# A decoder layer on one core: the first attention runs its token tiles two together instead of one after another

## The reference, cut to what matters

```python
# forgetting attention, 6 heads of 64 ("f"), for tokens t of a tile and all s <= t
s = q @ k.T * scale + cum[t] - cum[s];  o_f = softmax(s) @ v
# sparse attention, 6 query heads on 2 kv heads: three branches, each softmaxed by itself, gated and added
o_c = p_c @ vc                 # "c": 31 compressed keys
o_s = softmax(q @ k_slc.T * scale - slope * dist) @ v_slc    # "s": all blocks are selected at 512 tokens
o_w = softmax(q @ k_win.T * scale - slope * dist) @ v_win    # "w": window of 512
o = g0 * o_c + g1 * o_s + g2 * o_w
# all heads side by side, then the output projection
x = x + concat(o_f, o_pool, o) @ w_out
```

## Time and profile before

| what | us |
|---|---|
| median of 3 runs (815.58 to 817.59) | 815.82 |
| the profiled execution, its own time | 814.84 |
| its span (first to last instruction) | 813.0 |
| attention, first score to first matmul of the output projection | 156.49 to 259.92 |

### The profile page before, as it was taken

One profiled execution on the slowest core, in us unless ns is written; L12 is line 12 of the kernel. 1 busy time (PEld: TensorE's weight loads), 2 busy tenths in 40 slices (PEclk: granted clock), 3 DMA queues, 4 the chain that ended last, 5 costly groups with the idle time before them and its releaser, 6 DMA issues.

```text
span 813.0 us, 11870 instructions
## 1 busy us (share of the span) xinstructions
PE 765.6 (94%) x4244; PEld 595.0 (73%) x4244; DVE 534.8 (66%) x734; ACT 464.6 (57%) x697; POOL 181.2 (22%) x173
## 2 busy tenths in 40 slices
PE   3999999999999999999999986999999999999991
PEld 3978789666676889888798866677777777777761
DVE  4445346476677345632364289888899898899975
ACT  4455633376677315632353061687778887877852
POOL 2920000000000102000000010224555544455332
PEclk9999999999999999999999996999999999999996
DMA  9835440000006533553101767799999999999936
GB/s 291 228 86 151 135 130 2 0 1 2 1 2 201 188 129 107 190 196 101 55 1 52 266 235 294 289 394 371 386 385 380 370 381 373 375 387 382 384 106 220
DMA packets 61663, 167.23 MB, mean 206 GB/s; under 512 B 7926, under 2 KB 35894, under 8 KB 49334
## 3 DMA queue, kind: packets, MB, share of 16 engines
q1 hardware_dynamic: 56376, 150.69, 50.1%
q0 software_dynamic: 4240, 12.80, 6.7%
q10 hardware_dynamic: 1008, 3.21, 1.2%
HBM read 153.42 MB, written 13.24 MB: 205 GB/s over the span
## 4 chain that ended last, share of the span: by engine, by line
PE 52%; DMA 18%; POOL 10%; DVE 8%; issue 7%; ACT 4%; POOLq 1%; SPq 0%; ACTq 0%; DVEq 0%
DMA xod<-tok,yidx 16%; PE ps L1733 11%; PE ps L1735 11%; PE ps L1734 11%; POOL yidx L742 7%; PE ps L1941 5%; PE ps L1917 3%; PE ps L1981 2%; PE ps L1963 2%; PE ps L1936 2%; PE ps L1820 2%; POOL tok L753 1%; DVE wlo L1204 1%; POOL spare L750 1%; DVE wlo L1212 1%
## 5 line engine op out<-in xcount | busy, mean ns | idle before, releaser
L1204 DVE TENSOR_TENSOR wlo<-raw,whi 128x2048 fp32r<-128x2048 f32 x30 | 68.8, 2292 | 104.5 <-ACT whi L824 104.5
L1733 PE MATMUL ps<-whi,mhi 128*96 128x512 f32 (+1 forms) x288 | 114.2, 397 | 2.6 <-DVE mlo L1666 1.2
L1735 PE MATMUL ps<-whi,mlo 128*96 128x512 f32 (+1 forms) x288 | 113.6, 394 | 0.0
L1734 PE MATMUL ps<-wlo,mhi 128*96 128x512 f32 (+1 forms) x288 | 112.9, 392 | 0.0
L693 POOL TENSOR_SCALAR stat<-stat 128x1 f32<-128x1 f32 x18 | 11.5, 642 | 448.0 <-ACT tok L843 298.6
L1212 DVE TENSOR_TENSOR wlo<-arena,whi 128x2048 fp32r<-128x2048 f32 x40 | 91.5, 2291 | 14.9 <-ACT whi L837 14.9
L837 ACT ACTIVATE whi<-arena 128x2048 fp32r<-128x2048 f32 x40 | 76.7, 1917 | 28.6 <-PE ps L1735 28.6
L824 ACT ACTIVATE whi<-raw 128x2048 fp32r<-128x2048 f32 x30 | 57.3, 1910 | 62.3 <-PE ps L1735 62.2
L1733 PE MATMUL ps<-ahi,whi 128*128 128x512 f32 x192 | 76.2, 397 | 0.0
L1735 PE MATMUL ps<-ahi,wlo 128*128 128x512 f32 x192 | 75.3, 392 | 0.0
L1734 PE MATMUL ps<-alo,whi 128*128 128x512 f32 x192 | 75.3, 392 | 0.0
(11 more groups left out here) (334 smaller groups left out, 1657.6 us busy)
## 6 DMA issues: line engine op xcount, KB each, us to landing
arena<-in_exp_w_gate SPq DMA_DIRECT2D x30, 1024.0 KB, 18.0
arena<-in_exp_w_up SPq DMA_DIRECT2D x17, 1024.0 KB, 17.9
raw_a<-in_exp_w_down SPq DMA_DIRECT2D x16, 1024.0 KB, 20.1
raw<-in_exp_w_up SPq DMA_DIRECT2D x15, 1024.0 KB, 18.3
arena<-in_exp_w_down SPq DMA_DIRECT2D x9, 1024.0 KB, 21.9
raw<-in_exp_w_down SPq DMA_DIRECT2D x7, 1024.0 KB, 20.1
raw<-in_w_in SPq DMA_DIRECT2D x5, 1024.0 KB, 5.9
raw<-in_w_in SPq DMA_DIRECT2D x10, 512.0 KB, 5.7
```

The lines of the kernel that those rows point to most:

```text
L1204: v.tensor_tensor(wlo[:, n % SPLIT, :], raw[:, n % RAW, :], whi[:, n % SPLIT, :].bitcast(F32), ALU.subtract).then_inc(lo_done, 1)
L1733: mm(out_, ahi_, bhi_, start=first, stop=False)
L1734: mm(out_, ahi_, blo_, start=False, stop=False)
L1735: return mm(out_, alo_, bhi_, start=False, stop=last)
```

## The change

`TILES_A` becomes (3, 0, 2, 1), and the unit list is built for tiles 3 and 0 together, then for tiles 2 and 1 together. In each half the `f` pairs come first and alternate between the two tiles (two units of tile 3, two of tile 0, and so on), then all four `c` units, then for each pair of heads: s, s, w, w of the one tile and s, s, w, w of the other. The number of units, their instructions and their sizes stay. The bookkeeping that was written as arithmetic for one tile after another (`out_of`, `place`, the waits for a tile's outputs and for `PTc`) becomes tables made from the list: `jobs`, `spots`, `last_s`, `tile_outs`. The last `f` score is now unit 51 of 80 instead of unit 67. The lags (3 and 5 units) and the numbers of buffers are as before.

```diff
--- before.py
+++ after.py
@@ -244,7 +244,7 @@
         win, wout = A["w_in"][0], A["w_out"][0]
         wq, wk, wv, wo = (A[f"xattn_w{c}"][0] for c in "qkvo")
 
-        TILES_A = tuple(range(NT - 1, -1, -1))
+        TILES_A = (3, 0, 2, 1)
         pieces = []
         groups = []
         KEY = {}
@@ -355,9 +355,10 @@
 
 
         UN = []
-        for i in TILES_A:
-            UN += [(i, "c", g, 0) for g in range(NSA_G)] + [(i, "f", h, i + 1) for h in range(FOX_H)]
-            UN += [(i, b, 2 * p + e, i + 1) for p in range(NSA_H // 2) for b in "sw" for e in range(2)]
+        for both in (TILES_A[0:2], TILES_A[2:4]):
+            UN += [(i, "f", 2 * p + e, i + 1) for p in range(FOX_H // 2) for i in both for e in range(2)]
+            UN += [(i, "c", g, 0) for i in both for g in range(NSA_G)]
+            UN += [(i, b, 2 * p + e, i + 1) for p in range(NSA_H // 2) for i in both for b in "sw" for e in range(2)]
         UX = [(i, "x", h, MT) for i in range(NT) for h in range(MEM_H)]
 
 
@@ -387,6 +388,14 @@
                 self.o_lo = sem(name + "_o_lo")
                 self.by = 2 if name == "A" else 1
                 self.njobs = n // self.by
+                pairs = [units[u] for u in self.of_s][1::2]
+                self.jobs, self.spots, self.last_s = [], [], {}
+                for j, (i, kind, h, nb) in enumerate(pairs if self.by == 2 else ()):
+                    if kind != "w":
+                        self.spots.append((i, h // 2 if kind == "f" else 5 + h // 2))
+                    if kind == "s":
+                        self.last_s[i] = j
+                    self.jobs.append((len(self.spots) - 1, kind != "w", kind != "s"))
                 self.outs = 6 if name == "A" else MEM_H
                 self.steps = len(units) + LAG_V + 1
 
@@ -401,10 +410,13 @@
 
                 if self.by == 1:
                     return j, True, True
-                i, r = divmod(j, 9)
-                if r < 3:
-                    return 6 * i + r, True, True
-                return 6 * i + 3 + (r - 3) // 2, r % 2 == 1, r % 2 == 0
+                return self.jobs[j]
+
+            def tile_outs(self, t):
+
+                if self.by == 1:
+                    return self.outs * (t + 1)
+                return max(q for q, (i, f) in enumerate(self.spots) if i == t) + 1
 
             def bank(self, q):
 
@@ -418,14 +430,11 @@
 
             def place(self, q):
 
-                i, p = divmod(q, self.outs)
-                if self.by == 2:
-                    i = TILES_A[i]
-                t = slice(i * P, (i + 1) * P)
                 if self.by == 1:
-                    return slice(2 * p, 2 * p + 2), t
-                f = p if p < 3 else p + 2
-                return slice(f, f + 1), t
+                    i, p = divmod(q, self.outs)
+                    return slice(2 * p, 2 * p + 2), slice(i * P, (i + 1) * P)
+                i, f = self.spots[q]
+                return slice(f, f + 1), slice(i * P, (i + 1) * P)
 
         PA = Phase("A", UN, 0)
         PX = Phase("X", UX, 72)
@@ -1017,8 +1026,8 @@
                         i, kind, h, nb = ph.units[u]
                         act.wait_ge(ph.tp_done, u + 1)
                         if kind == "c":
-                            if TILES_A.index(i) >= 2:
-                                act.wait_ge(ph.pv_done, 9 * (TILES_A.index(i) - 2) + 8)
+                            if i in TILES_A[2:]:
+                                act.wait_ge(ph.pv_done, ph.last_s[{2: 0, 1: 3}[i]] + 1)
                             dst, src = PTc[i % 2][h], ps[3 + u % 2][0:NSA_R * CMP_PAD, 0:P]
                         else:
                             s = ph.sidx[u]
@@ -1769,7 +1778,7 @@
                     if ORDER[n] in ("out0", "xo0"):
 
                         ph = PA if ORDER[n] == "out0" else PX
-                        pe.wait_ge(ph.o_lo, ph.outs * ((TILES_A.index(idx) if ph is PA else idx) + 1))
+                        pe.wait_ge(ph.o_lo, ph.tile_outs(idx))
                     if kind == "H":
                         tc = slice(idx * P, (idx + 1) * P)
                         h4, l4 = (x[:, n % SPLIT, :].rearrange("p (k n) -> p k n", k=KF) for x in (whi, wlo))
```

## The result

The changed kernel takes 818.34 us, the kernel before 815.46 in the same comparison (16 runs each): a ratio of 1.0041, with a 95% interval of 1.0027 to 1.0054, so 2.2 to 4.4 us slower, 3.3 by the ratio and 2.9 between the two medians. The forecast was 819.4, 3.6 slower.

The account below looks back on a forecast made before the run. PE, busy 94%, bounds the kernel, so only idle time could move. Waits summed to 9.15 us against 4.7 before, +4.5, but the step-by-step walk's +3.6 was taken: 815.82 + 3.6 = 819.4 us, range 815.9 to 821.5.

Parts of the forecast that it names:

- The walk of PE's steps: Attention, step by step from piece prices and three wait rules: ends at 107.0 us against 103.4 before, +3.6.
- Only idle time can move: Attention: PE's instructions stay, so only its idle time can change, 4.7 us in all before the change.
- Start, 1.2: First half's start: small third and fourth scores leave PE waiting 0.7 for a score bank and 0.45 for scaling.
- Rule C: Transposes of unit k-3 wait for unit k-5's copy out of the same bank, done behind the exponential of score k-2.
- rival 2: Attention: only scaling and score banks hold PE, not copies; ends at 105.1 us, +1.6, 817.4 in all; chance 0.18.
- Forgetting units, 0.9: First half's `f` units: waits of 0.5 at step 6 and 0.4 at step 11; a gain of about 1 us over before.
- Gap, 1.3: First half's four `c` units, steps 12 to 15, without scores: transposes 9, 10, 11 wait 0.15, 0.75, 0.4 us.
- Refill, 2.1: First half, steps 16 to 23 behind the `c` units: waits at steps 19 to 22 of 0.35, 0.65, 0.95, 0.15 us.
- Steady groups: `s` and `w` units: PE sets the pace, 11.03 us per first-half group plus waits of 0.2 and 0.15; second half none.
- Rival 1: Attention: mixing works as meant, only start and drain cost, 1.2 + 0.4 for 4.7: -3.1 us, 812.7; chance 0.07.
- Rival 3: Attention: the clock falls in the gaps, 1.5 us lost over 4 us, +3 for both on top, 822.4; chance 0.05.
- Rival 4: Behind the attention: something waits for a transfer, so the attention changes but the end doesn't move, 815.8; chance 0.06.

Follow-up runs that it names:

- e1: The changed kernel with three PSUM banks for the transposes and two for the outputs: attention 104.66 us, ratio 1.0016 to the kernel before.
- e3: The changed kernel with the four `c` units of each half ahead of its `f` units: attention 103.84 us, ratio 1.0002 to the kernel before.
- e4: The changed kernel with each half's `c` units spread, one ahead of each four `f` units and one behind the last: attention 105.60 us, ratio 1.0027.
- e2: The kernel before with three PSUM banks for the transposes and two for the outputs: attention 102.45 us, ratio 0.9989 to the kernel before.
- e6: The changed kernel with both `c` units first in each half and three transposition banks: attention 101.38 us, ratio 0.9987 to the kernel before.
- e5: The changed kernel with neighbouring tiles together (TILES_A = 3, 2, 1, 0): attention 105.20 us with the clock fallen inside, ratio 1.0009 to the kernel before.

## Why the prediction was right

The walk of PE's steps ended at 107.0; the attention took 106.93. The mechanism held: gaps and refills at the compressed units, with PE waiting for ACT's copies. That the end was met to 0.1 is luck beside that, for single terms miss by up to 0.4. By its steps:

- *Only idle time can move.* Held: 4244 matmuls in both, and all of +3.50 in the attention, carried on 1:1 (553.1 and 553.4 behind it).
- *Start, 1.2.* Held to 0.02 (fourth score and first transposes above).
- *Rule C.* Held: PE starts 0.05 behind the end of each copy in the four places shown. e1 shows it as a cause, not as a coincidence of times: with the third bank 2.27 us go. But in the two gaps they don't: there the scaling takes the copy's place, and only 0.37 are saved. e1 refutes rival 2 (+1.6 without the rule; from 103.4 to its 105.1 it is +1.7): its time is what e1 then took, 104.66.
- *Forgetting units, 0.9.* The waits at steps 6 and 11 are there, 0.50 and 0.39 by starts. But I called the mixing a gain of 1 us here, which no run isolates: a group of big, big, small, small takes 5.73 where no gap follows it (e3), 0.4 over the price of PE's pieces.
- *Gap, 1.3.* By starts 0.22, 0.61 and 0.38 at units 9, 10 and 11 against 0.15, 0.75 and 0.4, so 1.2. The second gap, 1.45: by starts 0.42, 0.74 and 0.21, so 1.4.
- *Refill, 2.1.* Measured 0.34, 0.48, 0.81, 0.07 (each from the mask's start plus 0.05 to the transposes' start), 1.7: the largest miss of a term. The second half's, 1.0: 0.88 in the same way. What was said of its cause, ACT and DVE run dry by the gap, holds only in part: where the changed kernel waits 1.14 by the listed waits, e4, without a gap, waits 1.03, and e3, where `s` and `w` follow directly, 0.58.
- *Steady groups.* A group of eight takes 11.43 in the first half (score 24 to score 32), walked 11.38 (11.03 + 0.2 + 0.15), and 11.02 in the second, walked 11.02.
- *Sum against walk.* The sum of waits, +4.5, was too high and the walk, +3.6, right, but for the reason given only in part. The terms measured above (start, `f` units, both gaps, both refills, steady groups) come to 8.1 where the sum has 8.65; so some 0.6 of the 0.9 are waits that were smaller, and turnovers at a PV that fall away are left for the rest.
- *Rival 1, faster by mixing.* Wrong here, and e2, e3 and e6 show what it would have taken. From the value transposition, compressed units first in each order, mixing goes 103.86 to 104.39 with two banks and 102.89 to 101.92 with three. So with the compressed units first the sign of the mixing hangs on the third bank: +0.53 becomes -0.97. The third bank alone, with them where the change puts them, leaves it at +2.21.
- *Rival 3, clock.* Wrong for this kernel: 1.00 in both halves, in every stretch of 4 us. But the mechanism exists: in e5's profile the clock did fall behind a gap, for about the 1.5 us that the rival charged for one. The section of the Trainium skill's "TensorE: Matmul & The Clock Gate" named in the prediction doesn't describe the changed kernel: twelve listed waits in the attention for seven before, and no fall. In e5 it fell once and came back; nothing swung to and fro.
- *Rival 4, hidden.* Wrong, see the first point. SP now loads x at 223.6, not at 246.0, and what follows the attention takes as long as before.
- *The range.* The reach of -0.5 to +5.5 around 815.82 is 815.3 to 821.3, not quite the 815.9 to 821.5 written down. The measured 818.34 is inside both.

What stays open: the 2.2 us between e2 and e1 go when the compressed units come first (e6 is 0.97 under e2), but how they divide into start, gap, refill and small scores beside big copies was read from starts, not isolated by a run of its own. How much the contrast of sizes costs rests on an estimate, since the clock fell in e5's one profile.

## What to carry to other kernels

Before interleaving large and small units in a software pipeline, look which resource the pipeline turns over by unit number: here, with two banks for the transposes, a small unit next to a big one left PE waiting for the big one's copy. One more bank took off 2.3 us; only together with moving the units without scores to the front did it turn the interleaving from a loss into a gain. A step that brings no new work (here the units without scores) leaves PE nothing to cover the waits with. It was cheapest ahead of everything else of its half, 3.0 us less than in the middle; spreading such steps saved 1.3. A hand walk of the steps, with starts instead of durations and one exactly met wait to anchor the rule, placed the end within 0.1 us, with single terms off by up to 0.4, while adding up waits was 0.9 off. And look at the clock in every profile before comparing stretches: e5's length fitted its theory only because the clock had fallen.

## What the runs showed of the hardware

The stretch before the attention, 142 to 146, stands behind some 5.5 us of 32-column matmuls. It stood at a granted 0.63 in the kernel before, at 1.00 in the changed one and, in e2's profile, at 0.50 up to 150 (columns as in the earlier trace rows):

```profile
142.00:146.00 4.00, 4.00 (x18) 3.81 (x18) 2.07 (x7) 0.52 (x1) 0.00 (x0) 0.50 0.02 4
146.00:150.00 4.00, 4.00 (x11) 3.13 (x10) 3.05 (x6) 0.52 (x1) 0.00 (x0) 0.50 0.00 0
```

e2's attention therefore began at 160.8 instead of 156.5. So its span is 816.3, 3.3 us over the kernel before, though its attention is 1.0 us shorter, and the same code ahead of the change differs by more than the change is worth from one execution to the next (155.8 in the changed kernel's profile). A span from one profile doesn't rank such kernels; the length of the stretch does.

The fall in e5 is the only one inside an attention here. Before it PE was busy 2.89 of 4 us (230 to 234), with the transposes of 234.00 the last to wait. The changed kernel has a stretch just as idle, and its clock stayed at 1.00:

```profile
179.00:183.00 4.00, 2.87 (x23) 2.13 (x21) 3.85 (x13) 3.37 (x13) 0.00 (x0) 1.00 0.01 2
```

So what decides between the two isn't shown by these runs.
